# A hybrid encoder layer: low-rank products of decay and rate from split fp32r operands, weights fetched per channel block

## The reference, cut to what matters

```
w_log = -softplus(-(w0[d] + tanh(wd[d]) @ w_up[d])) - 0.5      # [256 tokens, 64] @ [64, 1024]
decay = exp(-exp(w_log))
a     = sigmoid(a0[d] + ad[d] @ a_up[d])                       # [256, 64] @ [64, 1024]
k_dir = k * (1 + (a - 1) * k_a)
```

## Time and profile before

| | us |
|---|---|
| median of 3 runs (2313.61 to 2315.21) | 2313.67 |
| the profiled execution's own time | 2313.12 |
| its span in the trace | 2311.3 |
| PE busy | 2288.0 (99%) |
| DVE busy | 1503.8 (65%) |
| ACT busy | 1118.2 (48%) |
| POOL busy | 134.3 (6%) |

### The profile page before, as it was taken

The page is one execution under the profiler, slowest core; times in us unless marked ns, Lnnn a source line. Parts: engine busy times, 40 slices in busy tenths (PEclk is TensorE's granted clock), DMA queues, the critical chain, the costliest instruction groups (busy, mean ns, idle before and its releaser), DMA issues.

```text
span 2311.3 us, 32552 instructions
## 1 busy us (share of the span) xinstructions
PE 2288.0 (99%) x12207; PEld 1886.3 (82%) x12207; DVE 1503.8 (65%) x2022; ACT 1118.2 (48%) x1506; POOL 134.3 (6%) x209
## 2 busy tenths in 40 slices
PE   9999999999999999999999999999999999999998
PEld 7888888888888888778788888887888888888886
DVE  5766754566756665997984576656676664476665
ACT  6454443444444665554666444445444443444443
POOL 1000000000000001222012220000000000000000
PEclk9999999999999999999999999999999999999999
DMA  8666666666664857668778325765666666666654
GB/s 269 192 191 198 191 192 194 192 195 192 191 198 144 273 172 205 194 196 274 222 214 240 120 70 172 241 223 173 209 187 198 194 194 193 192 191 195 194 192 146
DMA packets 229970, 451.51 MB, mean 195 GB/s; under 512 B 23436, under 2 KB 26272, under 8 KB 228448
## 3 DMA queue, kind: packets, MB, share of 16 engines
q1 hardware_dynamic: 208016, 399.88, 57.3%
q0 software_dynamic: 11600, 45.31, 5.8%
q10 hardware_dynamic: 10240, 4.76, 0.8%
HBM read 427.35 MB, written 22.54 MB: 195 GB/s over the span
## 4 chain that ended last, share of the span: by engine, by line
PE 94%; DVE 3%; DMA 2%; ACT 1%; issue 0%; ACTq 0%; DVEq 0%; POOL 0%; POOLq 0%
PE ps L1703 29%; PE ps L1705 28%; PE ps L1704 28%; DVE wlo L1060 1%; PE ps L2131 1%; PE ps L2116 1%; PE ps L2073 1%; PE ps L2101 1%; PE ps L2117 1%; PE ps L2074 1%; DMA xin<-dif_dram 0%; PE ps L1769 0%; DVE h L1149 0%; PE ps L1938 0%; DMA raw<-in_w_in 0%
## 5 line engine op out<-in xcount | busy, mean ns | idle before, releaser
L1060 DVE TENSOR_TENSOR wlo<-raw,whi 128x1024 fp32r<-128x1024 f32 (+1 forms) x760 | 929.7, 1228 | 669.2 <-ACT whi L544 664.8
L544 ACT ACTIVATE whi<-raw 128x1024 fp32r<-128x1024 f32 (+1 forms) x760 | 800.9, 1058 | 901.3 <-PE ps L1705 853.5
L1703 PE MATMUL ps<-whi,uhi 128*128 128x512 f32 (+1 forms) x2272 | 894.6, 394 | 4.5 <-issue 1.6
L1705 PE MATMUL ps<-whi,ulo 128*128 128x512 f32 (+1 forms) x2272 | 884.0, 389 | 0.9 <-issue 0.9
L1704 PE MATMUL ps<-wlo,uhi 128*128 128x512 f32 (+1 forms) x2272 | 883.5, 389 | 0.0
L1703 PEld LDWEIGHTS ps<-whi,uhi 128*128 128x128 f32 x2272 | 426.4, 188 | 101.2 <-issue 11.0
L1705 PEld LDWEIGHTS ps<-whi,ulo 128*128 128x128 f32 x2272 | 426.4, 188 | 88.7
L1704 PEld LDWEIGHTS ps<-wlo,uhi 128*128 128x128 f32 x2272 | 426.8, 188 | 84.3
L1703 PE MATMUL ps<-whi,hthi 128*128 128x512 f32 x704 | 273.9, 389 | 0.0
L1704 PE MATMUL ps<-wlo,hthi 128*128 128x512 f32 x704 | 273.9, 389 | 0.0
L1705 PE MATMUL ps<-whi,htlo 128*128 128x512 f32 x704 | 273.9, 389 | 0.0
(11 more groups left out here) (309 smaller groups left out, 1395.6 us busy)
## 6 DMA issues: line engine op xcount, KB each, us to landing
raw<-in_ffn_w_gu SPq DMA_DIRECT2D x352, 512.0 KB, 4.4
raw<-in_ffn_w_down SPq DMA_DIRECT2D x176, 512.0 KB, 4.4
raw<-in_w_in SPq DMA_DIRECT2D x160, 512.0 KB, 4.5
raw<-in_w_out SPq DMA_DIRECT2D x32, 512.0 KB, 4.0
raw<-in_w_branch_a SPq DMA_DIRECT2D x16, 512.0 KB, 5.1
raw<-in_w_branch_b SPq DMA_DIRECT2D x16, 512.0 KB, 4.7
gate_dram<-gst_g POOLq DMA_DIRECT2D x8, 512.0 KB, 6.7
gbuf<-gate_dram POOLq DMA_DIRECT2D x8, 512.0 KB, 4.9
```

The source lines that it names most:

```text
L544: nc.scalar.activation(whi[:, s, :, 0:p.width], raw[:, s, :, 0:p.width], ACT.Copy).then_inc(hi_ready, 1)
L1060: V.tensor_tensor(wlo[:, s, :, 0:p.width], raw[:, s, :, 0:p.width], whi[:, s, :, 0:p.width].bitcast(F32), ALU.subtract).then_inc(lo_ready, 1)
L1703: mm(o, at, w_, start=(j == 0 and k == 0), stop=False)
L1705: return mm(o, bt, w_, start=False, stop=(j == p.slots - 1 and k == SB - 1))
```

## The change

Each engine keeps its list; these edits are made in it:

- `wup` and `aup` go. In their place `wraw` holds the float32 weights of one channel block only, twice (partitions 0 to 63 and again 64 to 127), for both directions and both products: 128 x 512 elements. Four DMAs of 64 partitions fetch a block (`lora_rows`). Block 0 comes from POOL, after the other parameters; blocks 1 to 7 are issued from ACT's queue: block 1 in step 0 of round 3 of the shift stretch, block b + 2 at the end of ACT's odd round 2b + 1.
- `w2` (one buffer, 128 x 512, fp32r) is made of it for each block: ACT copies all 128 partitions (`w2_high`), DVE overwrites partitions 64 to 127 with the remainder (`w2_low`). For block b + 1 both stand in the odd round 2b + 1: on ACT behind the two tanh, on DVE behind L1388.
- `xh` and `xl0`/`xl1` are the high and low parts of `lwa`, each on both halves of the partitions, direction 1 already reversed. They are made once in round 0 of the shift stretch (four ACT copies in step 1, four DVE subtractions in step 2, 64 x 512 each).
- `low_rank(m)` becomes four fp32r matmuls of 128 rows and 256 columns instead of two float32 ones of 64 rows, and waits for `w2_low` of its block.
- `lwa` becomes a view of `nst`; `N_PAR` and `GS_SPLIT` are moved up by the counts added.

```
+        X_HIGH, X_LOW, W2_HIGH, W2_LOW = 3, 2, (7, 9, 10, 11, 12, 13, 14, 15), range(4, 4 + NPAIR)
+        def lora_rows(b):
+            return [(wraw[LORA * i:LORA * (i + 1), :, k, :], w[0].rearrange("d r c -> r d c")[:, :, b * P:(b + 1) * P])
+                    for i in range(2) for k, w in enumerate((w_up, a_up))]
 # ACT
+            def w2_high(b):
+                act.wait_ge(c_in if b else par_in, 16 * (1 + 4 * b) if b else 16 * N_PAR)
+                nc.scalar.activation(w2[:, :, :, :], wraw[:, :, :, :], ACT.Copy).then_inc(lora_act, 1)
+            def load_lora(b):
+                act.wait_ge(gd_ready, W2_LOW[b - 1])
+                for dst, src in lora_rows(b):
+                    act.dma_start(dst, src).then_inc(c_in, 16)
 # ACT, shift stretch
+                    if c == 0 and i == 1:
+                        act.wait_ge(lora_act, 1)
+                        for d in range(2):
+                            for r in range(2):
+                                last = nc.scalar.activation(xh[LORA * r:LORA * (r + 1), d, :, :],
+                                                            lwa[LORA * d:LORA * (d + 1), :, ::1 - 2 * d], ACT.Copy)
+                        last.then_inc(lora_act, 1)
+                    if c == 1 and i == 3:
+                        w2_high(0)
+                    if c == 3 and i == 0:
+                        load_lora(1)
 # ACT, direction stretch
                 last.then_inc(za_act, 1)
+                if d and b + 1 < NPAIR:
+                    w2_high(b + 1)
                 act.wait_ge(ex_in, m + 1)
...
                 if m >= 2:
                     stage_out(m - 2)
+                if d and b + 2 < NPAIR:
+                    load_lora(b + 2)
 # DVE
+            def w2_low(b):
+                dve.wait_ge(lora_act, W2_HIGH[b])
+                r = slice(LORA, P)
+                V.tensor_tensor(w2[r, :, :, :], wraw[r, :, :, :], w2[r, :, :, :].bitcast(F32), ALU.subtract).then_inc(gd_ready, 1)
...
+                    if c == 0 and i == 2:
+                        dve.wait_ge(lora_act, X_HIGH)
+                        for d, xl in enumerate((xl0, xl1)):
+                            for r in range(2):
+                                k = slice(LORA * d, LORA * (d + 1))
+                                last = V.tensor_tensor(xl[LORA * r:LORA * (r + 1), :, :], lwa[k, :, ::1 - 2 * d],
+                                                       xh[k, d, :, :].bitcast(F32), ALU.subtract)
+                        last.then_inc(gd_ready, 1)
+                    if c == 2 and i == 1:
+                        w2_low(0)
...
                                            in1=rr[:, b, :], op0=ALU.mult, op1=ALU.mult).then_inc(bon_in, 1)
+                if d and b + 1 < NPAIR:
+                    w2_low(b + 1)
                 dve.wait_ge(ex_out, m + 1)
 # PE
-                rows = slice(LORA * d, LORA * (d + 1))
-                sgn = slice(None, None, -1) if d else slice(None)
-                mm(ps[:, 4 + m % 2, 0:T], wup[rows, b * P:(b + 1) * P], lwa[rows, 0, sgn], start=True, stop=True)
-                mm(ps[:, 4 + m % 2, T:2 * T], aup[rows, b * P:(b + 1) * P], lwa[rows, 1, sgn],
-                   start=True, stop=True).then_inc(za_mm, 1)
+                pe.wait_ge(gd_ready, W2_LOW[b])
+                for k in range(2):
+                    o = ps[:, 4 + m % 2, k * T:(k + 1) * T]
+                    mm(o, w2[:, d, k, :], xh[:, d, k, :], start=True, stop=False)
+                    last = mm(o, w2[:, d, k, :], (xl1 if d else xl0)[:, k, :], start=False, stop=True)
+                last.then_inc(za_mm, 1)
 # POOL
-            pool.dma_start(wup[:, :], w_up[0].rearrange("d r c -> (d r) c")).then_inc(par_in, 16)
-            pool.dma_start(aup[:, :], a_up[0].rearrange("d r c -> (d r) c")).then_inc(par_in, 16)
...
+            for dst, src in lora_rows(0):
+                pool.dma_start(dst, src).then_inc(par_in, 16)
```

More of the change, by code:

```diff
@@ L268, in layer @@
         s_proj.close()
+        s_x, (_, xl0) = room(("x_gap", [P, QSLOTS * C + (NM - 2) * T]), ("xl0", [P, 2, T], F32R))
+        s_x.close()
         s_q, (q, beta, pend) = room(("q", [P, QSLOTS, C]), ("beta", [P, NM, T]), ("pend", [P, NM, NC_]))
-        s_rk, (rr, kr, kkn, wup, aup, lwa) = room(
+        s_rk, (rr, kr, kkn, xh, xl1, w2, wraw) = room(
             ("rr", [P, NPAIR, T]), ("kr", [P, NPAIR, T]), ("kkn", [P, NPAIR, T]),
-            ("wup", [P, RW]), ("aup", [P, RW]), ("lwa", [P, 2, T]))
+            ("xh", [P, 2, 2, T], F32R), ("xl1", [P, 2, T], F32R), ("w2", [P, 2, 2, P], F32R), ("wraw", [P, 2, 2, P]))
         bst, vb1 = (q[:, QSLOTS - 8 + 4 * i:QSLOTS - 4 + 4 * i, :].rearrange("p c t -> p (c t)") for i in range(2))
@@ L279, in layer @@
             ("kds", [P, T]), ("dst_a", [P, 2, NT, CW]), ("nst", [P, 2, NC_, C]))
+        lwa = nst[:, :, :, :].rearrange("p i c t -> p i (c t)")
         s_e.close()
@@ L394, in by_head @@
             return a.rearrange("p (g v) -> p g v", v=C)
-        N_PAR, GS_SPLIT = 8, 2
+        N_PAR, GS_SPLIT = 10, 3
         def slot_of(p, u, j):
@@ L1904, in _ @@
                             pe.wait_ge(par_in, 16 * N_PAR)
-                            pe.wait_ge(lora_act, GS_SPLIT + 4)
+                            pe.wait_ge(lora_act, W2_HIGH[0] + 1)
                         kk_spread(2 * i)
@@ L1910, in _ @@
                             pe.wait_ge(kk_ready, NPAIR)
-                            pe.wait_ge(gd_ready, 2)
+                            pe.wait_ge(gd_ready, X_LOW + 1)
                         g_product(2 * i)
@@ L1943, in _ @@
             pe.wait_ge(g_st, NPAIR)
-            pe.wait_ge(lora_act, 1)
+            pe.wait_ge(gd_ready, X_LOW)
             pe.wait_ge(sh_y, NBLK)
```

## The result

| | before | after |
|---|---|---|
| median, us | 2314.14 (4 runs, 2313.61 to 2315.21) | 2368.56 (4 runs, 2366.55 to 2372.01) |
| profiled execution, us | 2313.12 | 2372.01 |
| its span, us | 2311.3 | 2370.2 |
| granted clock over the span | 0.999 | 0.985 |

The ratio is 1.0231, 95% interval 1.0218 to 1.0243: 54 us slower in the medians, 59 us in the profiled executions (the one of after is the slowest of its four). The prediction was 2362 us.

What follows compares the result with a forecast made beforehand. PE, busy 99% of the span, was taken as the bound. From 2313.1 us, 39.2 for the direction stretch, 0.7 elsewhere, less 0.1 (+39.8), and 9 for the clock gave 2362 us; 8-in-10 range 2343 to 2375.

Steps and rivals of the forecast that it cites:

- The new wait: Direction stretch: PE's low_rank(2b + 2) waits for DVE's w2_low(b + 1) at seven places, 4 to 8 us each.
- δ: Added delay of DVE's even round from ACT's four DMA issues before its tanh: 2.0 us, 1.0 in round 2, bounds 0 and 2.6.
- the chain: Direction stretch: summed round times from low_rank(2) to low_rank(14), 145.55 us; low_rank(14) 39.67 late, result +39.2 us.
- rival B: Direction stretch: the waits come but the clock stays up, 2353 us (2344 to 2356); chance 0.27.
- The clock: Direction stretch: PE restarts at half rate after five of the seven new waits, 1.8 us each, +9 us.
- C: Direction stretch: slow level lasts a slot or more after each wait (19 us), δ at its upper bound, 2375 us; chance 0.11.
- A: Main forecast: waits in the direction stretch and slow clock restarts, 2362 us (2355 to 2371); chance 0.55.
- PE's own work: Direction stretch: each of 14 low_ranks 0.59 us cheaper, plus 0.1; 8.4 us won if PE stayed the bound everywhere.
- DVE's pace: Direction stretch: DVE paces the rounds, a cheaper low_rank only waits longer; nearly all of PE's 8.4 us is swallowed.
- Rival D: Direction stretch: wait hidden, DVE the bound, its added 4.8 us eat PE's gain, 2311 to 2316 us; chance 0.03.
- Elsewhere: Shift stretch, round 0: ACT's four added copies make PE wait about 0.7 us, bounds 0 and 2.5; the rest 0.
- After the stretch nothing gives time back: Behind the direction stretch: PE is full and all engines hang on its slots, so no lost time is recovered.

Runs made afterwards that it cites:

- The moved version: Changed kernel with w2_high, w2_low and the fetch of the next blocks one round earlier, in round 2b: 2320.93 us (1.0027).
- The run with a busy PE: Changed kernel with 36 fp32r matmuls, their sum never read, issued by PE before each of the seven waits for w2_low: 2357.92 us (1.0185).
- the doubled odd products: Changed kernel with the four matmuls of each odd low_rank from round 3 on done twice: 2367.22 us (1.0221).
- w2 made once: Changed kernel with w2 made for block 0 only and used for all eight blocks, later fetches left out: 2314.76 us (0.9995).
- POOL's order and aa moved: Kernel before, with aa made by ACT instead of DVE and POOL's even-round multiplications put before its wait for bonus: 2314.65 us (1.0000).
- the last one: Version with both moves and aa on ACT, plus POOL's even-round multiplications put before its wait for bonus: 2307.55 us (0.9969).
- that with aa on ACT: Version with both moves, plus one DVE operation of each round (aa = 0.5 tz + 0.5) made by ACT: 2313.08 us (0.9988).
- that with both moves: Changed kernel with w2_high and w2_low one round earlier and the fetches on POOL's queue in even rounds: 2320.27 us (1.0021).

## Why the prediction was right, by its steps

**The new wait: right.** Seven waits, DVE's w2_low named. The moved version shows that the place is the cause: w2_low in DVE's round 2b + 1 against PE's need at the end of its round 2b. From the end of an odd round's slots to the next waiting low_rank the forecast had 16.2, 16.3, 16.3, 17.2, 17.2, 17.2 us (rounds 2 to 12), and the trace has 17.0, 16.4, 16.4, 17.5, 17.6, 17.5: 102.3 in all against 100.4. The first wait ended at 939.13, forecast 939.41. n_products waited 3.5 us for POOL in rounds 4 and 6, as forecast.

**δ: right in kind, a little low.** An issue takes 0.63 us, at the upper end of the bounds, so round 2's 1.0 should have been about 1.6; the 2.0 of the later rounds was 2.1 to 2.2. One sum here was wrong: with δ = 0 the chain's own terms give 39.2 - 11 = +28, not +31, which would have put the low end of rival B and of the range 3 us lower. The run with the loads off ACT agrees: from the first n_products to the last it takes 11.3 us less than the kernel after.

**The clock: right in kind, the size too small.** Five of seven restarts at 1.8 us were taken, 9 us. From low_rank to the end of the slots behind it the seven places took 7.5, 11.5, 11.2, 11.1, 7.8, 8.7 and 10.3 us, against 0.7 + 2.73 a slot by the forecast: 14.1 us more in all, 1.3 to 2.6 at each of the seven. The run with a busy PE takes 15.1 us off at these places. Rival B (clock stays up, 2353) falls. C took the clock's price at 19, and 14.1 lies midway between it and the 9 of A: the profiled execution, 2372.0, is just above A's own range (2355 to 2371), the median, 2368.6, inside it. The Trainium skill's rule ("TensorE: Matmul & The Clock Gate", "Part 1: The HAM clock gate (the "warmup" mystery)"), that an idle PE goes back to half rate, agrees with the granted clock of 0.74 to 0.96 in this stretch and the 0.42 us spacing.

**PE's own work: the mechanism right, the size a little low, and right that it is swallowed.** A low_rank gives 0.58 us in even rounds and 0.79 in odd ones, 9.4 to 9.6 in all, where the forecast had 0.59 and 8.4. Two errors stand against each other in it: the four matmuls take 0.57 to 0.66 us between the others and not 0.47, and the matmuls around them, which were not counted, are spaced closer. That the gain is lost in the kernel after was argued from DVE's pace; the doubled odd products (nothing lost) show it.

**DVE's pace: underrated outside the kernel after.** With the waits gone I still expected 2307 for w2 made once and got 2314.8. From the first n_products to the last DVE was busy 130.4 of 140.4 us (19.52 of 20 at its fullest), and with w2 made once 131.5 of 137.6: little room for 8 us less of PE. Rival D had said so and I had not carried it over to the experiment.

**Elsewhere.** The 0.7 us at the shift stretch did not come: PE's transposes behind the four copies start at 787.20 (787.17 before), the first low_rank at 921.86 (921.81 before). ACT's emptying of the bank came 1.97 us later than before (785.90 against 783.93), not 2.45, and ended at 787.15, just in time. "After the stretch nothing gives time back" held, but something more was lost: from the first matmul of the last n_products to the end of the span it is 3.8 us longer in the profiled execution of after than before (1126.81 to 2370.2 against 1071.70 to 2311.3). PE waits there 1.4 us before the products of the scan's inverse (L2022) and 0.7 before a transpose (L2038), and one 40 us stretch has a clock of 0.96. The experiments' traces are 0.6 to 4.9 us longer there than the trace of the kernel before, and 2.8 of it stand in the kernel before with POOL's order and aa moved, which has nothing of the change. So it is not shown that these microseconds belong to the change; what causes them was not tried.

So of the 10 us by which the profiled execution exceeds the forecast, 5 are the clock, 2 the chain of rounds, and the rest stands behind the stretch.

## What to carry to other kernels

When a shared buffer is refilled per block, compare, for each engine, the program round that makes it with the round whose end needs it: here work placed in the odd round instead of the even one cost 48 us, while the buffer could stay single. A wait of five to seven microseconds on PE cost 1.3 to 2.6 more in its restart; matmuls whose sum is never read, put in front of it, buy that back, as long as they do not outlast the wait. And a cheaper product on the busiest engine is worth little until the engine just behind it (DVE, busy 93% of the stretch) and its feeder (POOL) are relieved: the same 9.4 us of PE gave nothing in the time of the version with w2 made once, and 7 in the last one.

## What was not expected of the hardware

- The clock fell behind waits of only 1.9 to 2.1 us: in round 14 of the version with w2 made once (1.89 us), in round 1 of that with w2 one round earlier (1.89), in round 4 of that with aa on ACT (2.06) and in round 6 of that with both moves (2.13), each time for a loss of about 1.6 us. PE's timeline of the first:

```profile
1058.12 0.68 PE L1981 MATMUL ps<-q,beta 64*64 64x64 f32 x16 [1.89 <-issue]
...
1060.14 0.63 PE L1746 MATMUL ps<-wlo,uhi 128*128 128x512 f32 x1
1060.56 0.63 PE L1747 MATMUL ps<-whi,ulo 128*128 128x512 f32 x1
```

  The spacing goes to 0.42 only about 1.2 us after PE has resumed. A wait of 1.91 us in round 4 of the same trace was followed by slots spaced 0.23 throughout, and so were one of 1.91 in the trace with w2 one round earlier (round 14) and even one of 2.62 in that with both moves (round 4). Why the one and not the other was not tried.
- A DMA of 64 x 2 rows of 512 bytes costs ACT's queue 0.63 us, as much as one of 256 pieces of 256 bytes (0.64).
